# One projection piece of the last prompt head moved from the middle of its weave to the last step

## The reference

```
proj = u @ w_in
gate_b, gate_c, xin, q, k, v = jnp.split(
    proj, [CONV_CH, 2 * CONV_CH, 3 * CONV_CH, 3 * CONV_CH + DA_WIDTH, 3 * CONV_CH + 2 * DA_WIDTH], axis=-1)
conv_y, conv_new = short_conv(gate_c * xin, conv_w, conv_buf)
y_conv = gate_b * conv_y
s = jnp.einsum('bqhcd,bkhcd->bhcqk', q, k).astype(jnp.float32) * (DA_DIM ** -0.5)
s = jnp.where(mask, s, -jnp.inf)
p = jax.nn.softmax(s, axis=-1)
w = p[:, :, 0] - lam * p[:, :, 1]
attn = jnp.einsum('bhqk,bkhe->bqhe', w.astype(v.dtype), v)
attn = rmsnorm(attn, subln_g) * (1.0 - lam_init)
mixed = jnp.concatenate([y_conv, attn.reshape(b, s, DA_WIDTH)], axis=-1) @ w_out
```

## Time and profile before

| what | value |
| --- | --- |
| median of 3 runs | 2713.95 us (2713.72 to 2718.39) |
| the profiled execution's own time | 2713.39 us |
| its span in the trace | 2711.8 us |
| TensorE matmuls, busy | 2624.9 us, 97% |
| VectorE busy | 1248.7 us, 46% |
| ScalarE busy | 1021.7 us, 38% |
| GpSimd busy | 451.7 us, 17% |
| mean granted TensorE clock | 0.99 |

### The profile page before, as it was taken

One profiled execution on the slowest core, in us unless ns is written; L12 is line 12 of the kernel. 1 busy time (PEld: TensorE's weight loads), 2 busy tenths in 40 slices (PEclk: granted clock), 3 DMA queues, 4 the chain that ended last, 5 costly groups with the idle time before them and its releaser, 6 DMA issues.

```text
span 2711.8 us, 49478 instructions
## 1 busy us (share of the span) xinstructions
PE 2624.9 (97%) x20215; PEld 1875.8 (69%) x20215; DVE 1248.7 (46%) x2064; ACT 1021.7 (38%) x1886; POOL 451.7 (17%) x513
## 2 busy tenths in 40 slices
PE   8999899999999999999999999999999999999997
PEld 5666666655688668886566666667656886788765
DVE  5555532326744214445653444344477441144454
ACT  4454422225444213433443232324355441244332
POOL 4000023222122002212201011110101220122121
PEclk9999999999999999999999999999999999999998
DMA  7211369761211311134435232332412121111442
GB/s 250 61 40 47 102 218 347 242 220 53 74 63 46 87 33 63 63 113 117 116 82 94 53 94 64 82 85 65 150 51 69 63 59 59 32 63 48 141 132 86
DMA packets 257660, 266.15 MB, mean 98 GB/s; under 512 B 10668, under 2 KB 217810, under 8 KB 256796
## 3 DMA queue, kind: packets, MB, share of 16 engines
q1 hardware_dynamic: 231772, 166.10, 22.0%
q0 software_dynamic: 25088, 94.79, 9.9%
q10 hardware_dynamic: 576, 2.10, 0.2%
HBM read 227.45 MB, written 35.50 MB: 97 GB/s over the span
## 4 chain that ended last, share of the span: by engine, by line
PE 88%; DVE 6%; ACT 2%; DMA 2%; issue 2%; POOL 0%; DVEq 0%; SPq 0%; ACTq 0%; POOLq 0%
PE ps L371 47%; PE ps L1115 25%; PE ps L1919 2%; PE ps L1907 1%; PE ps L1605 1%; PE ps L1958 1%; PE ps L1684 1%; PE ps L2454 1%; DVE arena L872 1%; PE ps L2434 1%; PE ps L2468 1%; DMA out<-hT 1%; DVE hT L876 1%; DVE w_split L344 1%; PE ps L1670 1%
## 5 line engine op out<-in xcount | busy, mean ns | idle before, releaser
L371 PE MATMUL ps<-u,w_split 128*128 128x352 f16 (+1 forms) x4752 | 752.2, 315 | 9.9 <-DVE u L736 5.9
L371 PEld LDWEIGHTS ps<-u,w_split 128*128 128x128 f16 (+1 forms) x4752 | 462.3, 98 | 259.7 <-issue 20.3
L371 PE MATMUL ps<-arena,w_split 128*128 128x352 f16 x3663 | 561.7, 314 | 3.7 <-DVE w_split L344 1.5
L371 PEld LDWEIGHTS ps<-arena,w_split 128*128 128x128 f16 x3663 | 358.1, 98 | 201.4 <-issue 9.4
L1115 PE MATMUL ps<-hT,w_split 128*128 128x264 f16 x3456 | 400.6, 276 | 3.2 <-ACT arena L1155 3.2
L1115 PEld LDWEIGHTS ps<-hT,w_split 128*128 128x128 f16 x3456 | 337.7, 98 | 55.0 <-DVE w_split L344 2.1
L344 DVE SCALAR_TENSOR_TENSOR w_split<-w_raw,w_split 128x1024 f16<-128x1024 f32 (+2 forms) x133 | 184.5, 1389 | 290.0 <-ACT w_split L328 289.4
L1115 PE MATMUL ps<-u,w_split 128*128 128x264 f16 x2592 | 303.4, 276 | 0.0
L1115 PEld LDWEIGHTS ps<-u,w_split 128*128 128x128 f16 x2592 | 253.6, 98 | 38.3
L328 ACT ACTIVATE w_split<-w_raw 128x1024 f16<-128x1024 f32 (+2 forms) x133 | 155.7, 1172 | 146.8 <-PE ps L371 99.0
L342 DVE SCALAR_TENSOR_TENSOR w_split<-arena,w_split 128x512 f16<-128x512 f32 x126 | 85.9, 725 | 103.9 <-ACT w_split L322 103.9
(11 more groups left out here) (398 smaller groups left out, 2983.6 us busy)
## 6 DMA issues: line engine op xcount, KB each, us to landing
w_raw<-in_w_down SPq DMA_DIRECT2D x58, 704.0 KB, 4.8
w_raw<-in_w_in SPq DMA_DIRECT2D x56, 512.0 KB, 7.9
arena<-in_w_gu SPq DMA_DIRECT2D x18, 1024.0 KB, 5.2
w_raw<-in_w_gu SPq DMA_DIRECT2D x18, 1024.0 KB, 5.2
hT<-in_cache_k SPq DMA_DIRECT2D x64, 256.0 KB, 4.3
hT<-in_cache_k POOLq DMA_DIRECT2D x64, 256.0 KB, 4.5
hT<-in_cache_v SPq DMA_DIRECT2D x64, 256.0 KB, 5.1
hT<-in_cache_v POOLq DMA_DIRECT2D x64, 256.0 KB, 5.4
```

Of the source, the lines that this page charges most:

```text
L371: ins = pe.matmul(ps[0:m, bank, 0:GW], split_of(v, wp)[:, k * w + col * P:k * w + col * P + m], x[:, xp, k0 + k, cols(g)], start=(k == 0 a ...
```

## The change

A second table is added. It is used by the three engines' streams for the last head alone; the three others keep the old one.

```diff
         HEAD_FILL = (0,) + (1,) * 5 + (1, 0) * 3 + (1, 1) + (1, 1, 0) * 4
+        LAST_FILL = (0,) + (1,) * 5 + (1, 0) * 2 + (0, 0) + (1, 1) + (1, 1, 0) * 3 + (2, 1, 0)
...
-                woven(act_head(act, h), act_proj0(act, 3 * h + 3, 3 * h + 5), HEAD_FILL)
+                woven(act_head(act, h), act_proj0(act, 3 * h + 3, 3 * h + 5), HEAD_FILL if h < HEADS - 1 else LAST_FILL)
...
-                woven(dve_head(dve, chain, h), dve_proj0(dve, chain, 3 * h + 3, 3 * h + 5), HEAD_FILL)
+                woven(dve_head(dve, chain, h), dve_proj0(dve, chain, 3 * h + 3, 3 * h + 5), HEAD_FILL if h < HEADS - 1 else LAST_FILL)
...
-                woven(pe_head(pe, h), pe_halves(pe, range(9 * h + 9, 9 * h + 18), u), HEAD_FILL)
+                woven(pe_head(pe, h), pe_halves(pe, range(9 * h + 9, 9 * h + 18), u), HEAD_FILL if h < HEADS - 1 else LAST_FILL)
```

## The result

The changed kernel takes 2717.23 us (median of 20 runs, 2713.12 to 2720.53), the kernel before 2712.65 us (median of 20 runs, 2707.69 to 2721.88). The ratio is 1.0016 with a 95% interval of 1.001 to 1.0023: the change costs some 4.3 us, between 2.7 and 6.2 us. That is under the 0.2% (5.4 us) that was taken as the bound of a visible difference, yet over twenty runs it is clear of noise: the bound was too coarse. The forecast was 2715.4 us with a range of 2711.5 to 2719.5 us.

What follows compares the result with a forecast made beforehand. TensorE's idle time was taken to bound the kernel: 3.36 us removed, 1.7 and 3.1 us added, 1.4 us more. From 2713.39 us that gives 2714.8, plus 0.56 for the median: 2715.4 us, range 2711.5 to 2719.5 us.

Steps and rivals of the forecast that it cites:

- What bounds the kernel: TensorE bounds, with 88% of the chain; the question is when PV(7) starts, and the steps after it keep their length.
- Block 2 loses its cover: Ahead of PV(2), TensorE idles about 1.7 us for ScalarE's copy; priced as one piece, 1.79 us.
- Blocks 3 to 5 cost nothing: In blocks 3 to 5, VectorE's mix(4) comes some 0.5 us later with 2 us of cover left; cost zero.
- Ta(6) and Ta(7): TensorE's waits for VectorE's mix ahead of these transposes, 2.66 and 0.70 us, both go.
- PV(6): a new wait of 3.1 us: Ahead of PV(6), TensorE waits 3.1 us for VectorE's copy of Tb(6), queued behind maxima, split, taps and product.
- The sum of 1.4 us: Idle time at PV(7): 3.36 us removed, 1.7 and 3.1 us added; PV(7) starts 1.4 us later.
- the term for the clock: Behind the new wait at PV(6), the forecast took no clock fall; a fall would cost 1.7 us.
- The clock: A clock fall behind PV(6) was possible, since 3.41 us of idling brought one and 2.66 us did not.
- the prediction's own sign: Wrong if the clock falls between 268 and 302 us, PV(6) waits 2 us or less, or PV(7) comes before 306 us.
- main case: Last head 1.4 us slower by idle time with no clock fall, 2715.4 us; chance 0.55.
- The rival that carried it, the clock rival: The clock falls behind the wait at PV(6): 3.1 us slower, 2717.1 us; chance 0.22.

Runs made afterwards that it cites:

- dve_split_late: Changed kernel, but on VectorE alone both pieces of block 6 come behind mix(7); ratio to the kernel before 0.9997 (0.9987 to 1.0007).
- vec_reorder: Kernel before, with VectorE's last head alone putting the second piece behind the mix in blocks 5 and 6; ratio 0.9991, run again 0.9996.
- cover_only: Changed kernel, but the piece taken from T(2) goes behind PV(2) and later pieces stand as before; ratio to the kernel before 1.0007 (0.9996 to 1.0018).
- change_look: The changed kernel unedited, traced again for the clock; single execution 2716.61 us.
- change_look2: The changed kernel unedited, traced once more for the clock; single execution 2718.65 us.
- piece_to_block6: Changed kernel, but the piece taken from block 2 goes behind Ta(6), one block earlier, on three engines; ratio to the kernel before 0.9996 (0.9984 to 1.0009).

## Why the prediction was right, and where it fell short

**What bounds the kernel.** Right. The change is worth what it does to TensorE's idle time and clock. The tail behind PV(7) kept its two waits, 2.88 us ahead of L1620 and 1.83 us ahead of L1920, as before. Its length it kept in two of four traces; in the other two the clock fell in it and it was 1.5 us longer, which the prediction did not consider.

**Block 2 loses its cover.** Right: 1.77 us of waiting for ScalarE's copy, where about 1.7 us was said.

**Blocks 3 to 5 cost nothing.** Right: no wait of TensorE stands between PV(2) and PV(6).

**Ta(6) and Ta(7).** Right: both waits are gone.

**PV(6): a new wait of 3.1 us.** Right in place, cause and size. It measured 3.09, 3.08, 3.08 and 3.08 us. dve_split_late shows the cause.

**The sum of 1.4 us.** Right as the effect of idle time: 4.86 - 3.36 = 1.5 us by the idle column of the table. As a forecast of the whole it was too small, since the term for the clock was put at nothing.

**The clock.** This is the step that failed. Between the wait of 3.41 us with a fall behind it and that of 2.66 us without one, I took the second for the likelier model of a wait of 3.1 us, and gave the fall 0.22. It came in four traces of four and costs 1.2 to 1.5 us beyond the idle time in the stretch. By the prediction's own sign, a fall of the clock in this stretch, its main case is wrong there. The argument against it, that the work around PV(6) is dense, did not hold. The rival that carried it (the clock falls behind the new wait, 3.1 us more) is what happened, as far as the stretch goes. That its time of 2717.1 us lies so near the measured 2717.23 us is in part luck: the forecast started from a median of three runs, 2713.95 us, and over twenty runs the kernel before takes 2712.65 us, so the measured loss is 4.3 us and not 3.1 us.

The rule of the Trainium skill, TensorE: Matmul & The Clock Gate, "The HAM clock gate", that idleness puts the clock back to half, spoke against this change. At this wait the traces agree: in each of the four, one stretch behind the 3.1 us of idle time is at 0.50 to 0.54. They do not at every wait of this size, as the last section shows.

**What stays open.** The stretch explains 2.7 to 3.0 us. The measured ratio says 4.3 us, with 2.7 us at the lower end of its interval. Part of the rest may be the tail: its fall of the clock adds 1.5 us in two of four traces of the changed kernel and in none of four of before, so that from PV(2) to L1920 the change is 3.0 to 4.3 us longer, 3.6 us on average. That the change makes this fall more frequent is not shown, two of four against none is too few. Nor is it seen further down: from PV(7) to the end of the trace the kernel before takes 2403.9 to 2408.6 us and the changed one 2402.8 to 2407.2 us, with falls at places that differ from one execution to the next. What is left is inside the interval.

**Chances and range.** The forecast of no difference over 0.2% held, and so did the range. That is less than it sounds: the bound of 5.4 us and the range of 8 us were wide enough for the main case and for the clock rival alike. The sign was right, the size was a third of what was measured.

## What to carry to other kernels

Filler work that is moved out of one step moves every piece behind it too, and with the pieces the work that other engines do for them. Here the wait for VectorE that was removed at Ta(6) came back at PV(6), because the same queue of split and taps had only changed sides. Follow the helper engine's stream from the edit to the end of the region, before counting a removed wait as a gain. It can be cheaper to reorder that engine alone: vec_reorder took 2.35 us out of the stretch and uncovered nothing, though a gain in the whole execution is not shown. And count the longest single wait apart from the sum of waits: 4.9 us with one wait of 3.1 us brought a fall of the clock in the stretch in four traces of four, 3.9 us in three parts did not in the one trace there is. Last, compare stretches between two instructions: without a fall of the clock this one repeats to 0.01 us, while whole executions spread by 7 us and more.

## What was not expected of the hardware

A fall of the granted clock is not fixed by the length of one wait. The same 2.66 us left the clock at 1.00 in four traces of the kernel before, and had 0.62 and 0.52 in the two stretches behind it in cover_only, where the instructions around it are the same ones. Behind 3.1 us it fell in four traces of four.

Two more waits stand in all thirteen traces. At or directly behind the 2.88 us ahead of L1619 (L1620, L1621) the clock fell in five of them: change_look, change_look2, piece_to_block6 and both of vec_reorder. At the 3.4 us that the earlier trace rows show it fell in twelve, but not in the first trace of vec_reorder, where the stretch from 256 to 260 us is at 1.00:

```profile
255.66 0.63 PE L1620 MATMUL ps<-ident,arena 128*128 128x128 f32 x4 [3.42 <-DVE arena L1789]
```

```profile
256.00:260.00 4.00, 4.00 (x29) 2.32 (x28) 1.62 (x3) 1.37 (x3) 0.00 (x0) 1.00 0.00 0
```

So a fall is to be given a chance that grows with the wait, from one in five at 2.66 us to nearly always at 3.1 and 3.4 us, and not a yes or no. What stands around these waits differs, and these counts are small.
